# A hybrid decoder step on one core: VectorE's work in a new order, level products computed in blocks, and five small changes of order

## What is computed

```python
# HGRN2, chunks of 64, 4 heads:  b = cumsum(log f)
A = einsum('bhtk,bhsk,bhtsk->bhts', qc, kc, exp(b_t - b_s), t >= s)
o = einsum('bhts,bhsv->bhtv', A, vc) + ...
# sparse attention: indexer scores, the best keys kept
score = einsum('bth,bths->bts', iw, relu(dots))
sel = top_k(score, min(256, lk // 4))
# ... attention over sel; compressed / selected / window attention ...
m = sum(gates * einsum('blnc,ncd->blnd', ys, w_branch), axis=2)
y = x + m @ w_out
```

## Time and profile before

| | |
|---|---|
| median of 3 runs | 991.56 us (988.15 to 992.1) |
| the profiled execution | 992.23 us, of which the span is 990.6 us |
| mean granted TensorE clock | 0.986 |
| PE busy | 952.4 us (96%) |
| DVE busy | 480.5 us (49%) |
| ACT busy | 303.4 us (31%) |
| moved by DMA | 188.96 MB, mean 191 GB/s |

### The profile page before, as it was taken

How to read it: one execution, slowest core, us unless ns; L and a number is a source line. 1 busy time by engine, 2 the same in 40 slices (tenths; PEclk the granted TensorE clock), 3 DMA queues, 4 the chain that set the end, 5 groups by cost and what they waited for, 6 DMA issues and landing times.

```text
span 990.6 us, 16671 instructions
## 1 busy us (share of the span) xinstructions
PE 952.4 (96%) x6058; PEld 775.3 (78%) x6058; DVE 480.5 (49%) x1350; ACT 303.4 (31%) x657; POOL 132.4 (13%) x258
## 2 busy tenths in 40 slices
PE   8999998999999999999999999899999999899998
PEld 6888777987677777888888886698777767678887
DVE  4223588778656403124240345887786463041331
ACT  2135422236743113310121463222476321133000
POOL 0510000002023261000060000000020413600000
PEclk9999998999999999999999999999999999999999
DMA  7644417435279798334454434274341997952432
GB/s 260 201 159 167 156 49 294 171 121 194 80 242 381 251 386 286 114 128 160 138 186 135 148 137 163 111 278 147 139 171 43 352 361 267 380 204 89 169 128 87
DMA packets 56212, 188.96 MB, mean 191 GB/s; under 512 B 9154, under 2 KB 22850, under 8 KB 43586
## 3 DMA queue, kind: packets, MB, share of 16 engines
q1 hardware_dynamic: 42850, 138.56, 40.0%
q0 software_dynamic: 12992, 49.16, 13.1%
q10 hardware_dynamic: 288, 0.18, 0.1%
HBM read 177.47 MB, written 18.77 MB: 198 GB/s over the span
## 4 chain that ended last, share of the span: by engine, by line
PE 83%; DVE 6%; ACT 4%; DVEq 2%; DMA 2%; issue 2%; ACTq 1%; SPq 1%
PE ps L883 24%; PE ps L999 16%; PE ps L1335 9%; PE ps L1343 6%; PE ps L1228 5%; PE ps L1027 3%; PE ps L872 2%; PE ps L1306 2%; DMA arena<-in_win_k_dram 2%; PE ps L1139 2%; PE ps L1127 2%; PE ps L1207 1%; DVE top L1796 1%; PE ps L1107 1%; DVEq L1799 1%
## 5 line engine op out<-in xcount | busy, mean ns | idle before, releaser
L883 PE MATMUL ps<-hT,slab 128*128 128x264 f32 (+1 forms) x1184 | 273.5, 390 | 0.0
L883 PEld LDWEIGHTS ps<-hT,slab 128*128 128x128 f32 (+1 forms) x1184 | 225.8, 193 | 39.7 <-issue 2.4
L999 PE MATMUL ps<-hT,slab 128*128 128x264 f32 x768 | 179.6, 391 | 1.7 <-DVEq L2092 1.7
L999 PEld LDWEIGHTS ps<-hT,slab 128*128 128x128 f32 x768 | 143.7, 191 | 32.7 <-issue 3.3
L1355 ACT ACTIVATE arena<-ps 128x512 f32<-128x512 f32 (+21 forms) x152 | 69.7, 484 | 179.7 <-PE ps L883 70.1
L1335 PE MATMUL ps<-Y,slab 128*128 128x264 f32 x384 | 85.8, 387 | 0.0
L1335 PEld LDWEIGHTS ps<-Y,slab 128*128 128x128 f32 x384 | 73.2, 191 | 12.3
L1228 PEld LDWEIGHTS ps<-arena,w 128*128 128x128 f32 x512 | 58.4, 192 | 10.0 <-issue 6.6
L1747 DVE SCALAR_TENSOR_TENSOR arena<-arena,small 128x264 f32<-128x264 f32 x26 | 11.0, 488 | 110.7 <-ACT arena L1430 110.7
L1228 PE MATMUL ps<-arena,w 128*128 128x128 f32 x512 | 61.4, 279 | 0.0
L1343 PE MATMUL ps<-arena,slab 128*128 128x264 f32 x256 | 57.5, 387 | 2.3 <-DVEq L2232 2.3
(11 more groups left out here) (360 smaller groups left out, 1184.4 us busy)
## 6 DMA issues: line engine op xcount, KB each, us to landing
slab<-in_weights_dram SPq DMA_DIRECT2D x86, 1024.0 KB, 4.9
arena<-in_pages_kv_dram SPq DMA_DIRECT2D x64, 256.0 KB, 8.5
arena<-in_pages_kv_dram POOLq DMA_DIRECT2D x64, 256.0 KB, 6.6
arena<-in_pages_kv_dram POOLq DMA_DIRECT2D x64, 128.0 KB, 7.3
arena<-in_pages_kv_dram SPq DMA_DIRECT2D x64, 128.0 KB, 11.3
out_dram<-in_state_win_dram POOLq DMA_DIRECT2D x2, 4088.0 KB, 25.8
arena<-in_state_hgrn_dram SPq DMA_DIRECT2D x2, 2048.0 KB, 7.6
out_dram<-arena POOLq DMA_DIRECT2D x2, 2048.0 KB, 6.8
```

Source lines behind the costliest of these rows:

```text
L883: last = mm(ps[0:job[3], n % 2, 0:LT], v[:, k, job[2]:job[2] + job[3]], hT[:, k, :], start=(k == 0), stop=(k == KD - 1))
L999: last = mm(ps[:, bank, 0:LT], v[:, k, (d % 2) * 128:(d % 2) * 128 + 128], hT[:, k, :], start=(k == 0), stop=(k == KD - 1))
```

## The change

It has these parts, in the order of the program.

1. **Start.** Slab iq0 comes in four quarters, one for two k each, with the quarters of x between them. `first_pair` runs both products of iq0 together, k outermost. The sum of squares moves from the second projection to the third. VectorE adds squares between the weighted columns. Idle products at the start: 4, not 5.
2. **Index scores.** hq1's two projections and `key_scores(0)` change places with the dots; ScalarE's order follows.
3. **VectorE.** Both `top_keys` and the mask move from before the scans to behind the last merge, where 14 rounds stood. No round is left in the levels. 4 rounds stand before the states' update, 9 in the compressed stage, 19 in the pages stage, with best, sort, threshold and the comparisons behind them and `join(0)` to `join(3)` between them.
4. **Levels in blocks.** Levels 0 to 4 compute only the two 64x64 blocks on the diagonal, level 5 two 32x32 blocks, level 6 one 64x64 block. `merge` takes these areas: for levels 0 to 5 four pieces of 64 rows instead of two of 128, for level 6 two.
5. **Ln table.** ScalarE loads it behind the squares, ahead of `take(0)`.
6. **A mix moved up.** `mix(6)` comes before the wait for "scores".
7. **Output.** For the first four output blocks k is outermost, in banks 4 to 7; the other four use banks 0 to 3.

The diff without the plumbing of semaphores and slab layout:

```diff
-                        if name == "iq0" and i < 2:
+                        if name == "iq0":
                             sp.dma_start(dst, src).then_inc(iq_in[i], 16)
-                            if l == 0:
-                                x_columns(2 * i + 1)
-                            if l == 0 and i == 0:
-                                x_columns(2)
+                            if l == 0 and i < 3:
+                                x_columns(i + 1)
...
-            keep_busy(5, 5)
+            keep_busy(5, 4)
...
-                                if n == 1 and k == 3:
+                                if n == 2 and k == 2:
...
+                def first_pair():
+
+                    for k in range(KD):
+                        if k % 2 == 0:
+                            pe.wait_ge(iq_in[k // 2], l * 16 + 16)
+                        pe.wait_ge(xg_v.sem, xg_v(l, f"g {k}"))
+                        for n, job in enumerate(SLAB_OF["iq0"][2]):
+                            if l and k == 0:
+                                pe.wait_ge(nx_v.sem, nx_v(l - 1, f"x {4 + n}"))
+                            last = mm(ps[:, n, 0:LT], stationary("iq0", job, k), XG[:, k, :], start=(k == 0), stop=(k == KD - 1))
+                            if k == KD - 1:
+                                last.then_inc(proj_ready, 1)
...
-                for name in FRONT:
+                first_pair()
+                for name in FRONT[1:]:
...
                 pe.wait_ge(pidx_a.sem, pidx_a(l, "iw"))
                 pe.wait_ge(sidx_a.sem, sidx_a(l, "new"))
+                project("hq1", 0)
                 dots(2)
                 dots(3)
-                project("hq1", 0)
+                pe.wait_ge(sidx_v.sem, sidx_v(l, "iws"))
+                key_scores(0)
                 dots(4)
                 dots(5)
-                pe.wait_ge(sidx_v.sem, sidx_v(l, "iws"))
-                key_scores(0)
+                project("hq1", 1)
                 dots(6)
                 dots(7)
-                project("hq1", 1)
                 pe.wait_ge(pidx_a.sem, pidx_a(l, f"relu {NH - 1}"))
                 key_scores(1)
                 project("hi0")
...
+                def level_blocks(i):
+
+                    if i < 5:
+                        return [(h, h) for h in halves]
+                    if i == 5:
+                        return [(slice(r, r + 32), slice(r + 32, r + 64)) for r in (0, 64)]
+                    return [(halves[0], halves[1])]
...
                         for t in range(2):
                             for h in range(4):
-                                x = m[:, h, t * 128:t * 128 + 128]
-                                last = mm(ps[:, b + t, h * 128:h * 128 + 128], x, x, start=True, stop=True)
+                                for s, q in level_blocks(i):
+                                    x = m[:, h, t * 128 + s.start:t * 128 + s.stop]
+                                    y = m[:, h, t * 128 + q.start:t * 128 + q.stop]
+                                    last = mm(ps[s, b + t, h * 128 + q.start:h * 128 + q.stop], x, y, start=True, stop=True)
...
                 pe.wait_ge(sidx_v.sem, sidx_v(l, "left out"))
                 mm(ps[0:ROWS, 5, 32:33], K("seq_rows")[eight[3]], dropped[eight[3], NQ:NQ + 1], start=True, stop=True)
+                pe.wait_ge(dc_a.sem, dc_a(l, "c 2"))
+                mix(6)
                 pe.wait_ge(dc_a.sem, dc_a(l, "scores"))
                 for q in range(4):
                     last = mm(ps[0:ROWS, (0, 1, 2, 4)[q], 0:NQ], K("seq_rows")[eight[q]], dropped[eight[q], 0:NQ], start=True, stop=True)
                 last.then_inc(dc_p.sem, dc_p.mark("new"))
-                pe.wait_ge(dc_a.sem, dc_a(l, "c 2"))
-                mix(6)
...
-                pe.wait_ge(ga_v.sem, ga_v(l, "b 2 7"))
-                for d in range(KD):
+                mixed(NMIX - 1)
+                views = [arrived("o0"), arrived("o1")]
+                for k in range(KD):
+                    pe.wait_ge(ga_v.sem, ga_v(l, f"b 2 {k}"))
+                    for d in range(4):
+                        last = mm(ps[:, 4 + d, 0:LT], views[d // 2][:, k, (d % 2) * 128:(d % 2) * 128 + 128], mT[:, k, :], start=(k == 0), stop=(k == KD - 1))
+                        if k == KD - 1:
+                            last.then_inc(ga_p.sem, ga_p.mark(f"o {d}"))
+                for d in range(4, KD):
                     v = arrived(f"o{d // 2}")
-                    if d >= 4:
-                        pe.wait_ge(nx_v.sem, nx_v(l, f"x {d - 4}"))
                     for k in range(KD):
-                        last = mm(ps[:, d % 4, 0:LT], v[:, k, (d % 2) * 128:(d % 2) * 128 + 128], mT[:, k, :], start=(k == 0), stop=(k == KD - 1))
+                        last = mm(ps[:, d - 4, 0:LT], v[:, k, (d % 2) * 128:(d % 2) * 128 + 128], mT[:, k, :], start=(k == 0), stop=(k == KD - 1))
                     last.then_inc(ga_p.sem, ga_p.mark(f"o {d}"))
...
                 relus(0)
                 relus(1)
-                relus(2)
-                relus(3)
                 evacuate("hq1", 0)
-                for n in range(4, NH):
+                for n in range(2, 6):
                     relus(n)
                 evacuate("hq1", 1)
+                relus(6)
+                relus(7)
                 act.drain().then_inc(hg_a.sem, hg_a.mark("gates"))
                 act.wait_ge(hg_v.sem, hg_v(l, "f"))
                 A(D_, fT[:, :, 0:LP], ACT.Ln).then_inc(hg_a.sem, hg_a.mark("ln"))
...
                 A(HSQ, HO.rearrange("p h t -> p (h t)"), ACT.Square).then_inc(hg_a.sem, hg_a.mark("sq"))
+                A(spare[:, :], epsb[:, :], ACT.Ln)
                 take(0)
                 act.wait_ge(hg_p.sem, hg_p(l, "ss"))
...
-            for k in range(1, KD):
-                square_added(0, k)
+                if k > 1:
+                    square_added(0, k - 1)
+            square_added(0, KD - 1)
...
                 ve.drain().then_inc(sidx_v.sem, sidx_v.mark("new"))
-                top_keys(slice(0, 128))
                 ve.drain().then_inc(hg_v.sem, hg_v.mark("f"))
-                top_keys(slice(128, 384))
-                TS(msk, acc, taken, NEG, ALU.not_equal, ALU.mult)
-                ve.drain()
-                TT(msk, msk, causal, ALU.add)
-                ve.drain().then_inc(pidx_v.sem, pidx_v.mark("mask"))
                 ve.wait_ge(hg_a.sem, hg_a(l, "ln"))
...
                     ve.wait_ge(hg_p.sem, hg_p(l, "a diag" if i < 0 else f"a {i}"))
                     rest()
+                    if i < 0:
+                        areas = [(slice(0, 128), slice(0, 128))]
+                    elif i < 6:
+                        areas = [(h, h) for h in halves]
+                    else:
+                        areas = [halves]
                     for t in range(2):
-                        nc.vector.copy_predicated(AT[:, t, :, :], lvl[:, level:level + 1, :].to_broadcast([128, 4, 128]),
-                                                  ps[:, banks + t, :].rearrange("p (h t) -> p h t", h=4))
+                        for s, q in areas:
+                            w = q.stop - q.start
+                            nc.vector.copy_predicated(AT[s, t, :, q], lvl[s, level:level + 1, q].to_broadcast([s.stop - s.start, 4, w]),
+                                                      ps[s, banks + t, :].rearrange("p (h t) -> p h t", h=4)[:, :, q])
                     ve.drain().then_inc(hg_v.sem, hg_v.mark("a diag" if i < 0 else f"a {i}"))
...
                 for i in range(9):
                     if i < 8:
                         decays(i + 1)
-                    if 2 <= i <= 5:
-                        left_out([i - 2])
                     ve.wait_ge(hg_a.sem, hg_a(l, f"e {i}"))
...
                    K("own_32")[all4].unsqueeze(2).to_broadcast([96 + NS, NS, 128]), ALU.mult).then_inc(hg_v.sem, hg_v.mark("vd"))
-                left_out(range(4, 18))
+                top_keys(slice(0, 128))
+                top_keys(slice(128, 384))
+                TS(msk, acc, taken, NEG, ALU.not_equal, ALU.mult)
+                ve.drain()
+                TT(msk, msk, causal, ALU.add)
+                ve.drain().then_inc(pidx_v.sem, pidx_v.mark("mask"))
                 ve.wait_ge(hg_p.sem, hg_p(l, "qk"))
                 TT(dqk[all4], ps[all4, 2, 0:NS], K("own_32")[all4], ALU.mult).then_inc(hg_v.sem, hg_v.mark("dqk"))
-                left_out(range(18, 23))
+                left_out(range(0, 4))
...
                 TT(hbias[:, :], hS[:, :, 16], b1, ALU.add).then_inc(cp_v.sem, cp_v.mark("sum"))
-                left_out(range(23, 32))
+                left_out(range(4, 13))
...
                 nc.vector.reciprocal(nbs[0:120, :], nbs[0:120, :]).then_inc(cp_v.sem, cp_v.mark("nb"))
-                best_of_pairs()
-                sort_pairs()
-                threshold()
                 ve.wait_ge(cp_p.sem, cp_p(l, "o"))
...
+                left_out(range(13, 18))
+                join(0)
+                left_out(range(18, 28))
```

(11 more changed lines are left out.)

19 lines of the change are left out of this document (4 added, 15 removed).

## The result

The changed kernel takes **980.97 us** (median of 4 runs, 980.89 to 982.31); beside it the kernel before took 990.2 (988.15 to 992.1). The ratio is 0.9901, 95% interval 0.9879 to 0.9924. The forecast was 967 with 957 to 980: the direction was right, the size was not; 9 us came instead of 25. (The forecast starts from the one profiled execution, 992.2 us; from there it is 11.)

A forecast was written before the change was run, and what follows sets the result against it. TensorE, busy 952 of 990.6 us, was taken to bound the kernel. From 992.2, -13.8 - 9.6 + 3.8 + 1.8 - 2.4 - 2.3 - 2.5 = -25.0 gave 967 us, range 957 to 980.

The forecast's parts named there:

- slabs o1 and iq1: Weight slabs for output and start, wanted some 7 and 3 us earlier; if late, they take back gain.
- The gap: TensorE's idle time before the first level and the lower clock behind it go, 6.9 us a layer: -13.8.
- Blocks side by side: In the levels the two output halves overlap, 1.1 us a level instead of 1.79: -9.6.
- rival 2: Blocks run one after another, levels 0 to 5 taking 2.0 us, not 1.1: +10.8, 978; chance 0.12.
- rival 2's milder form: Array drains at each change between half and full width in the levels: +4.8, 972; chance 0.08.
- VectorE in the levels: Four merge pieces cost 4 x 0.33, 1.33 us again; VectorE stays 0.3 under TensorE, cost 0.
- rival 3: Each merge piece costs as much as a whole, VectorE's cycle 5.6 us against 4.66: 980; chance 0.07.
- "left out": VectorE's 12.6 us tail behind the third join makes TensorE wait 3.3 us in layer 0, 0.5 in layer 1: +3.8.
- The clock behind it: Lower clock after the wait for "left out", counted as half such a loss: +1.8 (0 to 2.7).
- Rival 1: "left out" is in time, so neither its stall nor its clock is there: 961.5; chance 0.15.
- Start: Lost time before hT's first projection, 1.18 us of it waiting for VectorE, nearly all goes: -2.4 (0 to -3.1).

The follow-up runs named there:

- e2: Changed kernel with GpSimd's 4 MB window-state copy released by hq1's last product instead of level 0; 971.23 us, ratio 0.9784 to the kernel before.
- e9: Changed kernel with SyncE's 2 MB state load sent behind slabs g11 and g20, copy left at level 0; 972.96 us, ratio 0.9813 to the kernel before.
- e7: Changed kernel with part 4 undone: whole 128x128 products and merges in two pieces; 976.81 us, ratio 0.9834 to the kernel before.
- e5: Kernel before with only part 3 (VectorE's new order) of the change; 982.88 us, ratio 0.9928 to the kernel before.
- e6: Kernel before with only part 4 (levels in blocks, merges in pieces); 992.04 us, ratio 0.9991 to the kernel before.
- e11: Kernel of e4 with merges of levels 0 to 5 in two instructions over both tiles instead of four, level 6 in one; 958.75 us.
- e4: Changed kernel with three edits: VectorE's pages-stage tail early, window-state copy early, five idle products; 963.82 us, ratio 0.9704 to the kernel before.
- e1: Changed kernel with VectorE's pages-stage rounds, best, sort and threshold earlier, only comparisons behind join(2); 970.88 us, ratio 0.9778 to the kernel before.
- e3: Changed kernel with five idle products at the start instead of four; 980.8 us, ratio 0.9886 to the kernel before.
- e12: Kernel of e4 with one gate projection moved ahead of the level across the tiles, plus the merges of e11; 958.88 us.

## Why the prediction was wrong

- **The step that failed is the one that was not made**: the levels were priced on TensorE and VectorE alone, and the transfers in them were put at nothing without a reason. The prediction asked for slabs o1 and iq1 whether they would be wanted earlier, and did not ask it where the program gets 13 us ahead. What TensorE releases there (the 2 MB load, the 4 MB copy, slab g11) moved with it, closer together and closer behind the two slabs ahead of them. It cost 5.9 us of waits and 3.4 of clock, 9.3 of the 13.6 that were missing. e2, e9 and e7 show the cause: the waits go when either transfer is moved, and also when the levels are whole again. It takes both the closed gap, which slows the landing (e5: slow and in time), and the shorter levels, which bring the need closer. The row for it was in the trace of the kernel before: g11 took 16.9 us to land, with the copy beside it, and had 6.0 us to spare (185.1 against 191.1). Of these the faster levels took 2.7 (from its issue to its need 20.3 us instead of 23.0) and the longer landing 5.8; what is left, -2.5, is the stall of 2.53. The faster levels alone would have left it in time, as in e6, where it took 17.8 us.
- **The gap** was right in kind and near in size: 14.9 for 13.8. (4.75 + 4.91 us up to level 0 by the account, and 2 x 2.61 in the first level, 7.96 us for 5.35.) The missing 1.1 is mostly "flat" itself, 0.97 us at the lower clock and 0.54 now. e5 shows the gap closed alone.
- **Blocks side by side**: right; the serial case (rival 2) and rival 5 fall. The rule behind rival 2 (the Trainium skill, TensorE: Matmul & The Clock Gate, "Packing small matmuls") lets weight loads overlap running products only in another row group. The trace does not agree: here both blocks of a pair use all rows, in level 0 their loads start 7 ns apart and the next pair's some 58 ns later, while products of 222 ns run, and 32 records pass in 1.08 us. That the products would be serial was the prediction's inference from it. The term was still too large, 7.9 for 9.6 (a layer 5 x 0.51, 0.89 at level 5, 0.51 at level 6): I counted 0.1 for the change of width once, and the rows show 1.28 a level, 4.84 less the projection's 3.56: 0.94 for sixteen pairs and 0.34 for going in and out. The Trainium skill's rule that a change of mode drains the array (TensorEngine Tiling, "Key Properties") agrees with a cost at each change; rival 2's milder form had it up to 0.44.
- **VectorE in the levels** (rival 3) was wrong in its mild form: "halves by columns, 4 x 0.33". Whole tiles of 512 elements a row take 0.67 to 0.73, pieces of 256 took 1.82 / 4 = 0.46, e11's pieces of 64 rows and 512 elements 1.47 / 2 = 0.74. So at 64 rows 256 elements more cost 0.28, which leaves a fixed part of some 0.18 us a piece (an estimate from these two), and fewer rows save nothing. (The rival's own 14 x 0.9 should have been 14 x 0.98, 981.) It cost 0.5 us here and 2.8 more once the slab was in time (e2, e4, e9).
- **"left out"** was right in kind: 12.9 us of tail for 12.6. In layer 1 the wait came out at 3.59 for 0.5, since I took TensorE's need from an execution in which it had waited 2.6 us for window keys just before. The clock behind it came in both layers, not in half the cases. Rival 1 (in time) falls. e1 shows that the whole loss, 10 us, hung on the order of a few steps.
- **Start**: the wait for VectorE went as forecast, but the clock rose at 9.5 us, not at 6.3, and took 1.6 back (3.2 us at half pace); e3 leaves open how much of that is the fourth idle product.
- **The range** ended at 980 and the result is 981. The forecast had no case for a transfer that a faster engine releases too early, though it would have been a plain rival. That rivals 2 and 3 stood at 978 and 980, near the result, is chance: neither happened as priced. (The chances add up to 1.00 without the last 0.02.)

What stays open: why the clock falls where TensorE is busy, as at 280 us. The stretches stand at other places in every kernel (279 in the changed one, 305 in e4, 273 and 307 in e11, none there in e12). Most cost 1.7 us, some twice that (305 in e4, 273 in e11). In the profiled executions they sum to 12 us in the changed kernel, 6.3 in e4, 11 in e11 and 2.5 in e12, so they can make up the few us by which executions of like kernels differ.

## What to carry to other kernels

When an engine gets ahead of where it was, list what its progress releases, transfers above all, and compare for each the new time of need with issue plus landing time, in the company that it will have; the landing time in the old trace holds only for its company there (16.9 us became 22.7). A part of a change can have either sign by what surrounds it: the blocks cost 4 us beside a late slab and gained 7 without it, so undo the parts one by one. Long independent work on a helper engine goes where that engine was idle, ahead of the last thing that it waits for, not behind.

## What was not expected of the hardware

A small shift in when transfers start can cost far more than the shift. A 2 MB load took 7.6 us in the kernel before, 10.2 without the copy (e2), and 27.5 in the changed kernel beside a 4 MB copy within HBM, about as long as the copy itself (25.4 to 29.0). With load and copy 2.2 us apart it took 12.6 where the slabs ahead of it had landed before the copy began (e6) and 27.4 where they had not (e5). A 1 MB slab took 22.7, 18.1 with the copy alone and 6.2 without it. The products of 32 columns pass in 0.63 us for sixteen pairs, so products in a quarter of the output rows gain once more (level 5: 171.88 to 172.51). And a predicated copy of 512 elements a row takes 0.74 us over 64 rows and 0.67 to 0.73 over 128.
